# A hybrid streaming-encoder layer with 32 experts: large weights laid out in load order

## The reference, cut to what matters

```python
h = rms_norm(x, g_mix); proj = h @ w_in              # w_in (1024, 2304)
mkv = rms_norm(mem, g_mem) @ w_mem_kv                # (1024, 512)
x = x + concat(o_ret, o_swa, o_mem) @ w_out          # (1024, 1024)
# for every expert e, on the rows routed to it:
hu = xb @ w_up[e] + b_up[e]                          # w_up (32, 1024, 2048)
x_glu, x_lin = split(hu); x_glu = min(x_glu, 7); x_lin = clip(x_lin, -7, 7)
act = x_glu * sigmoid(1.702 * x_glu) * (x_lin + 1)
y = act @ w_down[e] + b_down[e]                      # w_down (32, 1024, 1024)
out = x + sum of gate * y over the token's experts
```

## Time and profile before

| what | us |
|---|---|
| runs | 1088.51, 1093.05, 1093.40 |
| median of the runs | 1093.05 |
| profiled execution, span from the first to the last instruction | 1090.2 |
| TensorE busy in it | 1000.7 (92%) |
| bytes moved by DMA in it | 422.74 MB, 388 GB/s over the span |

### The profile page before, as it was taken

The page is one execution under the profiler, slowest core; times in us unless marked ns, Lnnn a source line. Parts: engine busy times, 40 slices in busy tenths (PEclk is TensorE's granted clock), DMA queues, the critical chain, the costliest instruction groups (busy, mean ns, idle before and its releaser), DMA issues.

```text
span 1090.2 us, 11471 instructions
## 1 busy us (share of the span) xinstructions
PE 1000.7 (92%) x4559; PEld 412.2 (38%) x4559; DVE 240.1 (22%) x553; ACT 131.4 (12%) x241; POOL 12.3 (1%) x24
## 2 busy tenths in 40 slices
PE   8999999999999898899889898998889998989897
PEld 5446553443434232242424242433324242424233
DVE  2237242130303030211212030302112120303021
ACT  4117120101000000010100000000101000000000
POOL 0200000000000000000000000000000000000000
PEclk9999989999999999999999999999999999999999
DMA  9853859999999999999999999999999999999995
GB/s 344 305 205 130 320 204 393 368 412 421 419 421 419 422 421 419 422 419 423 419 422 419 423 419 423 421 420 421 420 421 421 421 421 421 419 422 421 420 422 207
DMA packets 67977, 422.74 MB, mean 388 GB/s; under 512 B 4925, under 2 KB 6358, under 8 KB 22902
## 3 DMA queue, kind: packets, MB, share of 16 engines
q1 hardware_dynamic: 67536, 422.06, 94.4%
q10 hardware_dynamic: 422, 0.41, 0.1%
HBM read 421.41 MB, written 1.05 MB: 388 GB/s over the span
## 4 chain that ended last, share of the span: by engine, by line
PE 43%; SPq 28%; DMA 24%; issue 2%; DVE 1%; ACT 1%; ACTq 0%
SPq L415 18%; PE psum L1321 13%; DMA ring<-in_w_up 12%; DMA work<-in_w_up 12%; PE psum L1365 11%; SPq L420 6%; PE psum L1051 4%; PE psum L1244 4%; SPq L426 4%; PE psum L1177 3%; PE psum L1006 2%; PE psum L1274 2%; PE psum L1043 1%; PE psum L1033 1%; PE psum L1234 0%
## 5 line engine op out<-in xcount | busy, mean ns | idle before, releaser
L1321 PE MATMUL psum<-ring,work 128*64 128x512 f32 x1520 | 352.1, 609 | 51.6 <-DMA ring<-in_w_up 50.7
L1321 PEld LDWEIGHTS psum<-ring,work 128*64 128x64 f32 x1520 | 106.5, 139 | 290.9 <-issue 208.1
L1365 PE MATMUL psum<-ring,work 128*64 128x512 f32 x752 | 165.1, 594 | 5.0 <-ACT work L655 2.8
L1321 PE MATMUL psum<-work 128*64 128x512 f32 x528 | 119.6, 597 | 18.8 <-DMA work<-in_w_up 18.8
L944 DVE TENSOR_TENSOR xy<-psum,xy 128x512 f32<-128x512 f32 x68 | 47.0, 692 | 233.7 <-PE psum L1274 233.7
L1365 PEld LDWEIGHTS psum<-ring,work 128*64 128x64 f32 x752 | 57.8, 137 | 101.0 <-issue 101.0
L648 ACT ACTIVATE work<-work 128x512 f32<-128x512 f32 x32 | 20.2, 630 | 577.3 <-DVE work L974 577.3
L893 DVE TENSOR_SCALAR work<-const 128x128 f32<-128x128 f32 x17 | 4.7, 279 | 362.1 <-PE psum L1234 362.1
L1321 PEld LDWEIGHTS psum<-work 128*64 128x64 f32 x528 | 35.4, 136 | 102.1 <-issue 62.5
L1274 PE MATMUL psum<-work 128*128 128x512 f32 x136 | 68.8, 631 | 2.2 <-issue 2.2
L1244 PE MATMUL psum<-work 128*128 128x128 f32 x544 | 65.0, 278 | 0.0
(11 more groups left out here) (169 smaller groups left out, 420.4 us busy)
## 6 DMA issues: line engine op xcount, KB each, us to landing
ring<-in_w_up SPq DMA_DIRECT2D x95, 2048.0 KB, 28.5
ring<-in_w_down SPq DMA_DIRECT2D x39, 2048.0 KB, 32.7
work<-in_w_up SPq DMA_DIRECT2D x32, 2048.0 KB, 28.3
work<-in_w_down SPq DMA_DIRECT2D x9, 2048.0 KB, 32.6
ring<-in_w_down SPq DMA_DIRECT2D x16, 1024.0 KB, 29.1
work<-in_w_down SPq DMA_DIRECT2D x16, 1024.0 KB, 28.9
ring<-in_w_in SPq DMA_DIRECT2D x4, 2048.0 KB, 19.8
ring<-in_w_out SPq DMA_DIRECT2D x2, 2048.0 KB, 10.0
```

Source lines behind the costliest of these rows:

```text
L1321: mm = pe.matmul(psum[r:r + SLOTS, n], XT[:, j, r:r + SLOTS], weights[e][:, n * N:(n + 1) * N], start=i == 0 and not first, stop=last, ski ...
L1365: mm = pe.matmul(psum[r:r + SLOTS, 4 + n], actT[:, 2 * i + k, r:r + SLOTS], weights[e][:, k * D + n * N:k * D + (n + 1) * N], start=i == 0 ...
```

## The change

The host lays out the large weights in the order in which they are loaded. Every chunk of 2 MB is then one contiguous block of HBM, and each partition receives one run of 16 KB from it, next to the run of the partition before it. The slots, the order of the loads, the waits and the sizes in bytes stay as they are.

In detail: w_up becomes (16 pairs, 8 chunks, 128, 4096), with the rows of both experts side by side. w_down becomes (16, 4, 128, 4096) with k outside and the expert inside, so that each half of the last chunk (k = 0, 1) is one run of 8 KB per partition. Row r of block k now lies in partition r, so the transposes of `sig` read 128 adjacent columns instead of every second one, and the down matmuls find expert e, half k at column (2k + e) D. w_mq is an input of its own, 8 KB per partition; w_in has four blocks, w_out two and w_mem_kv one, 16 KB per partition each. The two outside loads follow: the down chunk in one run of 16 KB, the up chunk in two DMAs of 8 KB runs as before.

```diff
-            sp.dma_start(w_mq_sb, w_in[0, :, 2048:2304].rearrange("(k p) n -> p k n", p=P)).then_inc(landed[2], 16)
+            sp.dma_start(ring[:, 2, 0:2048], w_mq).then_inc(landed[2], 16)
...
-                sp.dma_start(w_group_sb[n], w_in[0, :, n * N:(n + 1) * N].rearrange("(k p) n -> p k n", p=P)
-                             ).then_inc(landed[GROUP_SLOTS[n]], 16)
+                sp.dma_start(ring[:, GROUP_SLOTS[n], :], w_in[n]).then_inc(landed[GROUP_SLOTS[n]], 16)
...
-                    src = w_up[0, bass.ds(2 * p, 2), j * P:(j + 1) * P, :].rearrange("e r n -> r e n")
-                    sp.dma_start(slots[s].rearrange("r (e n) -> r e n", e=2), src).then_inc(landed[s], 16)
+                    sp.dma_start(slots[s], w_up[bass.ds(p, 1), j].rearrange("o r c -> (o r) c")).then_inc(landed[s], 16)
                     return
...
-                if i < DOWN_CHUNKS - 1:
-                    sp.dma_start(slots[s].rearrange("r (e n) -> r e n", e=2), src.rearrange("e (r k) n -> r e (k n)", k=2)
-                                 ).then_inc(landed[s], 16)
+                src = w_down[bass.ds(p, 1), j - UP_CHUNKS].rearrange("o r c -> (o r) c")
+                if j < PAIR_CHUNKS - 1:
+                    sp.dma_start(slots[s], src).then_inc(landed[s], 16)
                     return
-                src = src.rearrange("e (r k) n -> r e k n", k=2)
-                dst = slots[s].rearrange("r (e k n) -> r e k n", e=2, k=2)
                 for k, done in ((0, last_half_in), (1, landed[s])):
-                    sp.dma_start(dst[:, :, k], src[:, :, k]).then_inc(done, 16)
+                    half = slice(k * 2 * D, (k + 1) * 2 * D)
+                    sp.dma_start(slots[s][:, half], src[:, half]).then_inc(done, 16)
...
-                            sp.dma_start(outside_up[e], w_up[0, e, OUTSIDE_UP * P:(OUTSIDE_UP + 1) * P, :]
+                            sp.dma_start(outside_up[e], w_up[0, OUTSIDE_UP, :, e * 2 * F:(e + 1) * 2 * F]
...
-                        column = 256 * (j // 2) + j % 2
-                        mm = turn(psum[:, i, k * P:(k + 1) * P], sig[:, column:column + 255:2])
+                        mm = turn(psum[:, i, k * P:(k + 1) * P], sig[:, j * P:(j + 1) * P])
...
-                                               weights[e][:, k * D + n * N:k * D + (n + 1) * N],
+                                               slot[:, (2 * k + e) * D + n * N:(2 * k + e) * D + (n + 1) * N],
...
+def up_chunks(w):
+
+    e, d, n = w.shape
+    return w.reshape(e // 2, 2, d // P, P, n).transpose(0, 2, 3, 1, 4).reshape(e // 2, d // P, P, 2 * n)
+
+
+def down_chunks(w):
+
+    e, f, n = w.shape
+    return w.reshape(e // 2, 2, f // (2 * P), 2, P, n).transpose(0, 2, 4, 3, 1, 5).reshape(e // 2, f // (2 * P), P, 4 * n)
```

More of the change, by code:

```diff
@@ L102, in shape_constants, with layer_kernel @@
     return c
-def layer_kernel(nc, x, mem, positions, norm_gains, w_in, w_mem_kv, small_params, w_out, w_router, w_up, b_up,
+def layer_kernel(nc, x, mem, positions, norm_gains, w_mq, w_in, w_mem_kv, small_params, w_out, w_router, w_up, b_up,
                  w_down, b_down, constants, out):
@@ L110, in layer_kernel @@
     E = w_router.shape[2]
-    F = w_down.shape[2]
+    F = w_down.shape[1] * 2 * P
     TILES = S // P
@@ L395, in _ @@
                 sp.dma_start(xy[:, t], x[0, t * P:(t + 1) * P, :]).then_inc(x_in[t], 16)
-            sp.dma_start(w_mq_sb, w_in[0, :, 2048:2304].rearrange("(k p) n -> p k n", p=P)).then_inc(landed[2], 16)
+            sp.dma_start(ring[:, 2, 0:2048], w_mq).then_inc(landed[2], 16)
             for t in range(TILES):
                 sp.dma_start(mem_sb[:, t], mem[0, t * P:(t + 1) * P, :]).then_inc(mem_in[t], 16)
-            sp.dma_start(w_mem_sb, w_mem_kv[0].rearrange("(k p) n -> p k n", p=P)).then_inc(landed[0], 16)
+            sp.dma_start(ring[:, 0, :], w_mem_kv).then_inc(landed[0], 16)
             sp.dma_start(const[:, CONST_FIRST:], constants[:, CONST_FIRST:DIST_AT]).then_inc(tables_in, 16)
@@ L407, in _ @@
                 sp.wait_ge(slot_used, s + 2)
-                sp.dma_start(w_out_sb[s], w_out[0, :, s * N:(s + 1) * N].rearrange("(k p) n -> p k n", p=P)
-                             ).then_inc(landed[s], 16)
+                sp.dma_start(ring[:, s, :], w_out[s]).then_inc(landed[s], 16)
             def load(s, p, j):
                 if j < UP_CHUNKS:
-                    src = w_up[0, bass.ds(2 * p, 2), j * P:(j + 1) * P, :].rearrange("e r n -> r e n")
-                    sp.dma_start(slots[s].rearrange("r (e n) -> r e n", e=2), src).then_inc(landed[s], 16)
+                    sp.dma_start(slots[s], w_up[bass.ds(p, 1), j].rearrange("o r c -> (o r) c")).then_inc(landed[s], 16)
                     return
-                i = j - UP_CHUNKS
-                src = w_down[0, bass.ds(2 * p, 2), 2 * i * P:(2 * i + 2) * P, :]
-                if i < DOWN_CHUNKS - 1:
-                    sp.dma_start(slots[s].rearrange("r (e n) -> r e n", e=2), src.rearrange("e (r k) n -> r e (k n)", k=2)
-                                 ).then_inc(landed[s], 16)
+                src = w_down[bass.ds(p, 1), j - UP_CHUNKS].rearrange("o r c -> (o r) c")
+                if j < PAIR_CHUNKS - 1:
+                    sp.dma_start(slots[s], src).then_inc(landed[s], 16)
                     return
-                src = src.rearrange("e (r k) n -> r e k n", k=2)
-                dst = slots[s].rearrange("r (e k n) -> r e k n", e=2, k=2)
                 for k, done in ((0, last_half_in), (1, landed[s])):
-                    sp.dma_start(dst[:, :, k], src[:, :, k]).then_inc(done, 16)
+                    half = slice(k * 2 * D, (k + 1) * 2 * D)
+                    sp.dma_start(slots[s][:, half], src[:, half]).then_inc(done, 16)
             def pair(h, expert_h, u):
@@ L446, in first_pair @@
                         i = OUTSIDE_DOWN - UP_CHUNKS
-                        sp.dma_start(outside_down.rearrange("r (e n) -> r e n", e=2),
-                                     w_down[0, 0:2, 2 * i * P:(2 * i + 2) * P, :].rearrange("e (r k) n -> r e (k n)", k=2)
-                                     ).then_inc(outside_down_in, 16)
+                        sp.dma_start(outside_down, w_down[0, i]).then_inc(outside_down_in, 16)
                     elif c == 7:
@@ L1356, in pair @@
                         chunk_landed(pe, h, u, UP_CHUNKS + i, first)
-                    weights = [slot[:, e * 2 * F:(e + 1) * 2 * F] for e in range(2)]
                     for k in range(2):
@@ L1388, in _, with by_rows @@
                 last_share(PAIRS)
+def by_rows(w):
+    k, n = w.shape[0] // P, w.shape[1]
+    return w.reshape(k, P, n).transpose(1, 0, 2).reshape(P, k * n)
+def up_chunks(w):
[4 more added lines that the diff above has]
+    return w.reshape(e // 2, 2, f // (2 * P), 2, P, n).transpose(0, 2, 4, 3, 1, 5).reshape(e // 2, f // (2 * P), P, 4 * n)
 def kernel(**inputs):
@@ L1397 @@
     gains = [a[name].reshape(-1, P) for name in ("g_mix", "g_mem", "g_ffn")]
+    w_in = a["w_in"][0]
     params = [a[name] for name in ("swa_q_gain", "swa_k_gain", "mem_q_gain", "mem_k_gain", "swa_sinks", "b_router")]
@@ L1400 @@
         "x": a["x"], "mem": a["mem"], "positions": a["positions"].reshape(-1, P).T,
-        "norm_gains": np.concatenate(gains, 0), "w_in": a["w_in"], "w_mem_kv": a["w_mem_kv"],
-        "small_params": np.concatenate(params, 1), "w_out": a["w_out"], "w_router": a["w_router"],
-        "w_up": a["w_up"], "b_up": a["b_up"], "w_down": a["w_down"], "b_down": a["b_down"],
+        "norm_gains": np.concatenate(gains, 0), "w_mq": by_rows(w_in[:, 2048:]),
+        "w_in": np.stack([by_rows(w_in[:, n * 512:(n + 1) * 512]) for n in range(4)]),
+        "w_mem_kv": by_rows(a["w_mem_kv"][0]), "small_params": np.concatenate(params, 1),
+        "w_out": np.stack([by_rows(a["w_out"][0, :, n * 512:(n + 1) * 512]) for n in range(2)]),
+        "w_router": a["w_router"], "w_up": up_chunks(a["w_up"][0]), "b_up": a["b_up"],
+        "w_down": down_chunks(a["w_down"][0]), "b_down": a["b_down"],
         "constants": shape_constants(a["w_router"].shape[2]),
```

## The result

The changed kernel takes 1075.27 us (median of 4 runs, 1073.47 to 1075.45); the kernel before has a median of 1092.25 us over the 4 runs beside it. By the medians that is 17.0 us faster, where 15.0 had been forecast and 1078.0 us predicted. The ratio of the runs beside each other is 0.9855, with a 95% interval of 0.9838 to 0.9872: 15.8 us of 1092.25, between 14.0 and 17.7. The forecast lies inside this interval, so the 2 us between 15.0 and 17.0 are not clear of the noise. The profiled execution has a span of 1073.3 us against 1090.2.

What follows compares the result with a forecast made beforehand. The prediction took the weight stream to bound the expert stage. Fewer packets there save 14.6 us and the first load 0.4, together 15.0, taken from 1093.05 to give 1078.0 us; range 1073 to 1091.

Steps and rivals of the forecast that it cites:

- The bound: Expert stage: the weight stream sets 828 us at 59.80 us per pair of experts; TensorE alone needs 52.0.
- The price of a packet: Weight stream: 10.2 ns per contiguous run; 1664 fewer per pair save 1.06 us, over 13.8 pairs 14.6 us.
- The extrapolation to 16 KB: Weight stream: the price fitted at 2, 4 and 8 KB was taken to hold for 16 KB packets, one doubling off.
- the mixer's other loads: Ahead of the expert stage: w_in, w_mem_kv and w_out save 0.57 us each beside a busy TensorE, so nothing in time.
- The rule of 3 cycles: Trainium skill's fixed overhead per packet, an estimate of 3.5 ns against 10.2; the sum would be 5 us.
- The first load: w_mq at the kernel's start: 896 fewer packets let the first projection start 0 to 0.57 us earlier; 0.4 taken.
- The tail: From the last wait for a chunk to the end: 33.5 us that don't depend on the stream; no change expected.
- A part: Rival, weight stream: only part of the packet price goes; with a third of it, 1088 us; chance 0.14.
- Packets cut: Rival, weight stream: the descriptor generator cuts 16 KB runs into two 8 KB packets; 1090.5 us; chance 0.09.
- Addresses: Rival, weight stream: partitions 16 KB apart in HBM meet in the same memory banks more often; 1115 us; chance 0.09.

Runs made afterwards that it cites:

- 2 KB runs: The changed kernel with each partition's 16 KB per chunk split into eight runs of 2 KB, the chunk still one block of 2 MB: 1166.0 us, 1.0685 of before.
- a pitch of 128 KB: The changed kernel with the chunk index of w_up inside the partition, so that neighbouring 16 KB runs lie 128 KB apart: 1075.8 us, 0.9867 of before.
- The kernel with 8 KB runs: The changed kernel with each 2 MB chunk as two contiguous blocks of 1 MB in one place, two runs of 8 KB per partition: 1086.3 us, 0.9959 of before.
- a pitch of 2 MB: The changed kernel with the partition as outermost index of w_up, 16 KB runs of neighbouring partitions 2 MB apart: 1083.9 us, 0.9924 of before.
- only w_up: The changed kernel with w_down, its loads, strided transposes and down operands taken from the kernel before: 1081.9 us, 0.993 of before.
- two with doubles: The changed kernel with some chunk pairs loaded by one DMA (32 KB runs): four doubles, 1075.1 us; or three, only in the last 14 pairs, 1074.5 us.
- 4 KB runs: The changed kernel with each partition's 16 KB per chunk split into four runs of 4 KB, the chunk still one block: 1114.1 us, 1.0217 of before.
- four doubles: The changed kernel with up chunks 0+1, 2+3, 4+5 and down chunks 0+1 each loaded by one DMA from the second pair on: 1075.1 us, 0.986.

## Why the prediction was right, step by step

**The bound.** Right. The stream sets the pace; the pace went where the packets said, and TensorE's 52 us per pair left room.

**The price of a packet.** Right in kind, 9% too high: 10.2 ns from two stretches, of which one held only 1909 packets and 3.84 MB, known to three digits; 9.4 from the two whole traces. Per pair 0.99 us came instead of 1.06, in 13.8 pairs 13.7 us instead of 14.6. The extrapolation to 16 KB, the step least founded, held. That the mixer's other loads are fully covered is not contradicted: TensorE is busy 219.99 of the first 229 us in after and 219.72 in before.

**The rule of 3 cycles.** The estimate of 3.5 ns from the Trainium skill (DMA: Bandwidth & Descriptors, Why small descriptors are slow) gave 1088 us for this change and 1109 for 2 KB runs. 1075 and 1166 were measured. The trace doesn't agree with it for packets of 2 to 16 KB.

**The first load.** Its landing and its first user in after, answering to the earlier trace rows:

```profile
DMA to landing us min/median/max: 7.6/7.6/7.6
...
9.76 3.75 PE L1025 MATMUL psum<-ring,work 128*128 128x256 f32 x8 [0.84 <-issue]
```

Landing took 7.6 us instead of 8.2, and the first projection starts 0.63 us earlier; 0.4 had been taken, 0.57 was my upper end. Whether that lead lasts is not shown: the matmuls that begin at 350.12 in the trace of before begin at 349.81 in the first trace of the changed kernel, but at 352.30 in its second.

**Where 17 us come from.** In the profiles it is 16.9: the last wait for a chunk came 14.9 us earlier, the tail was 2.0 us shorter. Of the 14.9, 13.7 is the pace; 1.2 us are left, which lie before the stream runs freely. That stage in the kernel before, and then in the changed kernel run once more:

```profile
0.00:229.00 229.00, 219.72 (x894) 111.88 (x895) 74.83 (x215) 56.26 (x122) 12.30 (x24) 0.99 0.75 290
...
0.00:229.00 229.00, 220.83 (x885) 114.00 (x887) 75.04 (x215) 56.33 (x122) 12.30 (x24) 0.97 0.73 287
```

In the first profile of the changed kernel it is 292 GB/s; against 290 that is 0.5 MB, about 1 us of stream. But this is no effect of the change that the runs can show, as the second profile has only 287, at a granted clock of 0.97 instead of 0.99: there the last wait for a chunk ends at 1044.00 and not at 1041.80, and the span is 1075.4 us and not 1073.3. The profile with a pitch of 128 KB, at the same pace, has 297 GB/s and a span of 1069.2 us. So executions at one pace differ by up to 2.3 MB, some 5 us of stream, in what has been moved by 229 us, and a comparison of two profiles is no finer than that.

**The tail** I had put at nothing. In the profile of before the last share (L1274) takes 5.37 us, in the profiles of all eleven others 3.67 us, and the window around it in before has a granted clock of 0.68:

```profile
1080.00:1085.00 5.00, 3.39 (x4) 1.38 (x5) 0.69 (x1) 0.05 (x1) 0.00 (x0) 0.68 0.02 3
```

TensorE had been idle for 2.19 us ahead of it. The kernel with 8 KB runs idled for 2.26 us there and kept its clock, the one with 2 KB runs for 3.2 us. So the dip doesn't follow from that wait alone, and nothing in the change accounts for it. Whether it is in every execution of the kernel before stays open, as there is one profile of it. In these two profiles it is 1.7 of the 16.9 us. That the forecast of 15.0 came so close to 17.0 is in part luck: the pace was over-estimated by 0.9 us, the tail and the stage before 229 us, both put at next to nothing, gave 3.2 us in this pair of profiles, and with the second profile of the changed kernel the whole difference would be 14.8.

**The rivals.** "A part" would have needed a smaller c at 16 KB; it is the same. "Packets cut" is excluded by the count, 25366. "Addresses" is real at a pitch of 2 MB and absent at 16 and 128 KB.

## What to carry to other kernels

Where a stream of loads sets the pace, count its packets: here each run of contiguous bytes costs an engine 9.4 ns beside 36.7 ns per KB, so going from 8 KB to 16 KB runs (for one chunk in twelve from 4 KB to 8 KB) gave 1.7% of the pace and from 2 KB to 4 KB 6%. Fit both numbers to two saturated stretches with different run lengths, and take long ones: with 10 us of 2 KB runs the price came out as 10.2 ns, with whole traces as 9.4. Each further doubling saves half as much, while larger loads wait for more free slots and let the consumer wait in larger pieces; here nothing of the saving beyond 16 KB was left in the time (1075.1 and 1074.5 us against 1075.3).

## What the runs showed that I had not expected

The line with one price per packet fits eight packet mixes from 2 to 32 KB (before and after, to which it was fitted, three run lengths, only w_up, two with doubles) within 0.04% of the window. A pitch of exactly 2 MB between partitions costs a stream in which w_up lies so 0.9%, and 16 KB of padding removes it.

TensorE's clock dips after some of its waits for the stream. In before, the longest wait of each pair is the one at its first chunk, and in every second pair the matmuls after it are slow. Two consecutive pairs of before, and the stage table for the 5 us after the first wait, with its granted clock of 0.66:

```profile
483.77 8.78 PE L1321 MATMUL psum<-ring,work 128*64 128x512 f32 x32 [2.20 <-DMA ring<-in_w_up]
...
543.62 3.65 PE L1321 MATMUL psum<-ring,work 128*64 128x512 f32 x16 [2.17 <-DMA ring<-in_w_up]
...
483.77:488.77 5.00, 5.00 (x16) 1.48 (x18) 0.00 (x0) 0.00 (x0) 0.00 (x0) 0.66 1.01 421
```

The same wait in after, in two consecutive pairs:

```profile
478.22 3.65 PE L1313 MATMUL psum<-ring,work 128*64 128x512 f32 x16 [1.84 <-DMA ring<-in_w_up]
...
537.11 3.65 PE L1313 MATMUL psum<-ring,work 128*64 128x512 f32 x16 [1.78 <-DMA ring<-in_w_up]
```

After 2.20 us of idle, 32 matmuls take 8.78 us, where 7.07 is usual; after 2.17 they are not slowed. In before this happens in five pairs, at 483.77, 603.34, 722.91, 842.51 and 962.05, after 2.20 to 2.25 us each. In after no wait is longer than 1.9 us, and none is followed by it. Five times 1.71 us, and 1.7 us in the last share, are 10.2 of the 10.7 us by which TensorE's busy time fell (7.8 us in the second profile of the changed kernel). The kernel's time gained at most the last of them, since TensorE had slack in these pairs.

That the waits became shorter is not shown to be the reason. In before itself 2.22 us are harmless (782.82) and 2.20 us are not. With 8 KB runs in one block the slow pairs are those after 2.07 to 2.09 us (422.28, 541.56 and so on), while 2.12 to 2.17 us in the pairs between are harmless. With 4 KB runs the same wait is 2.80 to 2.88 us in every pair from 368 us on, and not one of these twelve is slow; with four doubles 3.96 us are harmless in one pair, and in the next 3.99 us are followed by slow matmuls (4 KB runs, then four doubles):

```profile
1044.48 3.65 PE L1318 MATMUL psum<-ring,work 128*64 128x512 f32 x16 [2.83 <-DMA ring<-in_w_up]
...
780.26 7.09 PE L1343 MATMUL psum<-ring,work 128*64 128x512 f32 x32 [3.96 <-DMA ring<-in_w_up]
...
838.66 8.78 PE L1343 MATMUL psum<-ring,work 128*64 128x512 f32 x32 [3.99 <-DMA ring<-in_w_up]
```

So the length of the wait alone doesn't decide, and what does stays open.
